# A fifth slot of 1 MB in the experts' weight stream, with the routing tables in the place of the gates

## What is computed

```python
def routed_moe(h, w_router, b_router, w1, w3, w2):
    scores = jax.nn.sigmoid(h @ w_router)
    sel = scores + b_router
    ...
    _, idx = lax.top_k(jnp.where(in_group, sel, -jnp.inf), TOP_K)
    ...
    for e in range(N_EXPERTS):
        y_e = (jax.nn.silu(h @ w1[e]) * (h @ w3[e])) @ w2[e]
        y = y + combine[:, e:e + 1] * y_e
    return y
```

## Time and profile before

| | |
|---|---|
| median of 3 runs | 948.19 us (947.85 to 950.93) |
| the profiled execution | 960.5 us |
| its span, first to last instruction | 958.9 us |
| its mean granted TensorE clock | 0.959 |
| busy PE / PEld / DVE / ACT / POOL | 829.1 / 697.1 / 623.5 / 516.7 / 230.7 us |
| moved by DMA | 209 MB, mean 218 GB/s |

### The profile page before, as it was taken

One profiled execution on the slowest core, in us unless ns is written; L12 is line 12 of the kernel. 1 busy time (PEld: TensorE's weight loads), 2 busy tenths in 40 slices (PEclk: granted clock), 3 DMA queues, 4 the chain that ended last, 5 costly groups with the idle time before them and its releaser, 6 DMA issues. The chain is left out here.

```text
span 958.9 us, 15876 instructions
## 1 busy us (share of the span) xinstructions
PE 829.1 (86%) x6374; PEld 697.1 (73%) x6374; DVE 623.5 (65%) x804; ACT 516.7 (54%) x814; POOL 230.7 (24%) x336
## 2 busy tenths in 40 slices
PE   4998997999889997897879889759999999999980
PEld 2777875898669875697668788648887777777760
DVE  2596764458544676245446465578988888888865
ACT  3475741457323752338343164367777777777751
POOL 3113150124201360013400110007323223223122
PEclk9999999999999999899989999869999999999995
DMA  9977478245943468438694248618999999999964
GB/s 312 268 239 195 123 168 207 62 117 148 211 115 84 137 154 187 117 78 256 184 248 127 67 141 279 242 44 300 340 348 354 360 357 370 372 359 357 339 202 151
DMA packets 220052, 209.00 MB, mean 218 GB/s; under 512 B 51100, under 2 KB 156229, under 8 KB 219337
## 3 DMA queue, kind: packets, MB, share of 16 engines
q1 hardware_dynamic: 217241, 203.80, 68.6%
q0 software_dynamic: 2736, 4.15, 1.3%
HBM read 190.64 MB, written 23.10 MB: 223 GB/s over the span
## 5 line engine op out<-in xcount | busy, mean ns | idle before, releaser
L2038 DVE TENSOR_TENSOR w_lo<-raw,w_hi 128x2048 fp32r<-128x2048 f32 x96 | 232.1, 2428 | 39.4 <-ACT w_hi L1473 39.3
L2259 PE MATMUL bank<-hT,half_hi 128*128 128x256 f32 (+1 forms) x1024 | 228.6, 319 | 10.6 <-DVE half_lo L1593 4.3
L1473 ACT CAST w_hi<-raw 128x2048 fp32r<-128x2048 f32 x96 | 183.3, 1912 | 71.0 <-DMA raw<-in_w_e_dram 65.6
L2259 PEld LDWEIGHTS bank<-hT,half_hi 128*128 128x128 f32 x1024 | 167.2, 192 | 26.9 <-issue 7.8
L2259 PE MATMUL bank<-w_hi,window 128*128 128x512 f32 x480 | 157.7, 399 | 3.0 <-DVE w_lo L2038 3.0
L2259 PE MATMUL bank<-hT,half_lo 128*128 128x256 f32 (+1 forms) x512 | 159.6, 312 | 0.0
L1593 DVE TENSOR_TENSOR half_lo<-half_raw,half_hi 128x1024 fp32r<-128x1024 f32 x88 | 108.6, 1236 | 59.3 <-ACT half_hi L1033 58.8
L2259 PE MATMUL bank<-lane 64*64 64x64 f32 (+2 forms) x2096 | 103.9, 240 | 22.0 <-issue 10.7
L2259 PEld LDWEIGHTS bank<-lane 64*64 64x64 f32 (+2 forms) x2096 | 95.3, 151 | 33.5 <-issue 18.6
L2259 PEld LDWEIGHTS bank<-w_hi,window 128*128 128x128 f32 x480 | 90.2, 188 | 28.0 <-issue 6.6
L1033 ACT CAST half_hi<-half_raw 128x1024 fp32r<-128x1024 f32 x88 | 92.2, 1049 | 26.7 <-DMA half_raw<-in_w_out_dram 8.0
(11 more groups left out here) (321 smaller groups left out, 1285.3 us busy)
## 6 DMA issues: line engine op xcount, KB each, us to landing
raw<-in_w_e_dram SPq DMA_DIRECT2D x96, 1024.0 KB, 7.4
half_raw<-in_w_in_dram SPq DMA_DIRECT2D x64, 512.0 KB, 5.0
half_raw<-in_w_ada_dram SPq DMA_DIRECT2D x32, 512.0 KB, 4.9
raw<-in_w_ada_dram SPq DMA_DIRECT2D x8, 1024.0 KB, 10.7
dense<-staged SPq DMA_DIRECT2D x32, 128.0 KB, 4.4
half_raw<-in_w_proj_a_dram SPq DMA_DIRECT2D x8, 512.0 KB, 5.4
half_raw<-in_w_proj_b_dram SPq DMA_DIRECT2D x8, 512.0 KB, 4.0
half_raw<-in_w_out_dram SPq DMA_DIRECT2D x8, 512.0 KB, 8.7
```

The costliest lines, as they stand in the source:

```text
L1473: act.copy(e_hi[n % WBUF][:, :], raw[n % RING][:, :]).then_inc(s["hi_ready"], 1)
L2038: dve.tensor_tensor(e_lo[n % WBUF][:, :], raw[n % RING][:, :], e_hi[n % WBUF][:, :].bitcast(F32), ALU.subtract)\
L2259: return nc.tensor.matmul(dst, lhsT, rhs, start=start, stop=stop)
```

## The change

The stream gets a fifth slot, `raw4`, of 8 KB on each partition, at the end of the memory. The room for it comes from the routing tables, which now lie over `gates`. In the stream, slot and landing semaphore of unit n are n % 5, SP waits for the split of unit n-5, and the counts of landings follow (`fills_until`). The first ring of eight loads at the kernel's start and the loop for overfull experts still use four slots; the latter's counts are adapted (`turn_fills`).

```diff
--- before.py
+++ after.py
@@ -5,6 +5,7 @@
 
 
 
+import math
 from contextlib import ExitStack
 
 import concourse.bass as bass
@@ -35,6 +36,7 @@
 DE = 512
 N = 512
 RING = 4
+SLOTS_AHEAD = 5
 SLOTS = P
 UNIT = 2048
 HALF = 1024
@@ -120,6 +122,7 @@
         hT_hi, hT_lo = hT[:, 0, :, :], hT[:, 1, :, :]
         ZO_AT = (nc.sbuf_base + 31) // 32 * 32
         zo = sb("zo", [P, 4 * D])
+        GATES_AT = (nc.sbuf_base + 31) // 32 * 32
         gates = sb("gates", [P, 8, TILES, HEADS, DIRS])
         gate_row = sb("gate_row", [P, 2, DIRS, HEADS])
         key_sq = sb("key_sq", [P, 4, TILES])
@@ -175,22 +178,34 @@
         act_hi = sb("act_hi", [P, 4, P], F32R)
         act_lo = sb("act_lo", [P, 4, P], F32R)
         y_out = [sb(f"y_out{g}", [P, D]) for g in range(2)]
-        both = sb("both", [P, 2, EXPERTS], BF16)
...
-        pair_weight = sb("pair_weight", [P, 2, 2])
+        routing_at = GATES_AT
+
+        def sb_routing(name, shape, dt=F32):
+            nonlocal routing_at
+            t = nc.alloc_sbuf_tensor_at(name, shape, dt, offset=routing_at)
+            size = (2 if dt == BF16 else 4) * math.prod(shape[1:])
+            routing_at += (size + 31) // 32 * 32
+            assert routing_at <= GATES_AT + 4 * 8 * TILES * HEADS * DIRS
+            return t
+
+        both = sb_routing("both", [P, 2, EXPERTS], BF16)
...
+        pair_weight = sb_routing("pair_weight", [P, 2, 2])
         y_tok = nc.alloc_sbuf_tensor_at("y_tok", [P, 2, 2, D], F32, offset=LANE_AT)
         window = [nc.alloc_sbuf_tensor_at(f"window{g}", [P, 2, KC, P], F32R, offset=LANE_AT + 8 * D * g) for g in range(2)]
         w_lo4 = nc.alloc_sbuf_tensor_at("w_lo4", [P, UNIT], F32R, offset=VEC_AT + 4 * D)
+        FIFTH_AT = (nc.sbuf_base + 31) // 32 * 32
+        slots = raw + [nc.alloc_sbuf_tensor_at("raw4", [P, UNIT], F32, offset=FIFTH_AT)]
         e_hi = [w_hi3, w_hi[0], w_hi[1], w_hi4]
         e_lo = [w_lo3, w_lo[0], w_lo[1], w_lo4]
 
@@ -319,7 +334,7 @@
             "gathered window_ready rows_placed silu_done act_done act_turned act_rounded act_split "
             "y_copied first_rows x2_ready x2_squared x2_power out_ready"
         ).split()}
-        landed = [sem(f"landed{r}") for r in range(RING)]
+        landed = [sem(f"landed{r}") for r in range(SLOTS_AHEAD)]
         half_landed = [sem(f"half_landed{r}") for r in range(HRING)]
         spilled = [sem(f"spilled{r}") for r in range(STAGES)]
         y_stored = [sem(f"y_stored{g}") for g in range(2)]
@@ -487,6 +502,14 @@
         TURN_AFTER = {3: ("back_copied", 2), 4: ("v_copied", 2), 5: ("k_normed", 3)}
         BACK_AFTER = {0: ("back_copied", 0), 1: ("back_copied", 1), 2: ("k_normed", 4), 3: ("back_copied", 3)}
         SLOT_FILLS = ADA_UNITS // RING
+
+        def fills_until(n):
+            r = n % SLOTS_AHEAD
+            return n // SLOTS_AHEAD + 1 + (SLOT_FILLS if r < RING else 0)
+
+        def turn_fills(k):
+            r = k % RING
+            return SLOT_FILLS + len([n for n in range(ALL_UNITS) if n % SLOTS_AHEAD == r]) + k // RING + 1
         e1_v = w_e1[0].rearrange("e (c p) n -> p (e c) n", p=P)
         e3_v = w_e3[0].rearrange("e (c p) n -> p (e c) n", p=P)
         e2_v = w_e2[0].rearrange("e (c p) n -> p (e c) n", p=P)
@@ -752,7 +775,7 @@
             sp.wait_ge(s["merged_split"], KC)
             def expert_turn(i):
                 for k, (v, q, half) in enumerate(TURN_UNITS):
-                    sp.wait_ge(s["unit_split"], i * PER_TURN + (ALL_UNITS + k - RING + 1))
+                    sp.wait_ge(s["unit_split"], i * PER_TURN + (ALL_UNITS + max(k - RING + 1, 0)))
                     if v is e2_v:
                         src = v[:, bass.ds(i * 8 + q * 4, 4), half * N:half * N + N]
                     else:
@@ -760,13 +783,13 @@
                     load(four(raw[k % RING]), src, landed[k % RING])
 
             for n, (v, q, half_) in enumerate(STREAM):
-                if n >= RING:
-                    sp.wait_ge(s["unit_split"], n - RING + 1)
+                if n >= SLOTS_AHEAD:
+                    sp.wait_ge(s["unit_split"], n - SLOTS_AHEAD + 1)
                 if v is e2_v:
                     src = v[:, 4 * q:4 * q + 4, half_ * N:half_ * N + N]
                 else:
                     src = v[:, 8 * q + 4 * half_:8 * q + 4 * half_ + 4, :]
-                load(four(raw[n % RING]), src, landed[n % RING])
+                load(four(slots[n % SLOTS_AHEAD]), src, landed[n % SLOTS_AHEAD])
             sp.wait_ge(s["h2_ready"], 2)
             load(ada_vec[:, 0, :], final_g.partition_broadcast(P), s["landed_final"])
             last_rows = slice(LISTED, FIRST_TURN)
@@ -1465,12 +1488,12 @@
             x_copy(0, 1)
 
             def expert_high(n):
-                act.wait_ge(landed[n % RING], 16 * (SLOT_FILLS + n // RING + 1))
+                act.wait_ge(landed[n % SLOTS_AHEAD], 16 * fills_until(n))
                 if n < 4:
                     act.wait_ge(s["half_used"], EXPERT_AFTER[n])
                 else:
                     act.wait_ge(s["unit_used"], n - WBUF + 1)
-                act.copy(e_hi[n % WBUF][:, :], raw[n % RING][:, :]).then_inc(s["hi_ready"], 1)
+                act.copy(e_hi[n % WBUF][:, :], slots[n % SLOTS_AHEAD][:, :]).then_inc(s["hi_ready"], 1)
 
             expert_high(0)
             x_squares(1, 0)
@@ -1539,7 +1562,7 @@
             def expert_turn(i):
                 def high(k):
                     act.wait_ge(landed[k % RING], i * (16 * PER_TURN // RING)
-                                + 16 * (SLOT_FILLS + ALL_UNITS // RING + k // RING + 1))
+                                + 16 * turn_fills(k))
                     act.wait_ge(s["unit_used"], i * PER_TURN + (ALL_UNITS + k - WBUF + 1))
                     act.copy(e_hi[k % WBUF][:, :], raw[k % RING][:, :]).then_inc(s["hi_ready"], 1)
 
@@ -2035,7 +2058,7 @@
 
             def expert_low(n):
                 dve.wait_ge(s["hi_ready"], n + 1)
-                dve.tensor_tensor(e_lo[n % WBUF][:, :], raw[n % RING][:, :], e_hi[n % WBUF][:, :].bitcast(F32), ALU.subtract)\
+                dve.tensor_tensor(e_lo[n % WBUF][:, :], slots[n % SLOTS_AHEAD][:, :], e_hi[n % WBUF][:, :].bitcast(F32), ALU.subtract)\
                     .then_inc(s["unit_split"], 1)
 
             def attended(chunk, t):
```

More of the change, by code:

```diff
@@ L177, in block_kernel @@
         y_out = [sb(f"y_out{g}", [P, D]) for g in range(2)]
-        both = sb("both", [P, 2, EXPERTS], BF16)
[L179 to L189, removed]
-        pair_weight = sb("pair_weight", [P, 2, 2])
+        routing_at = GATES_AT
[7 more added lines that the diff above has]
+        both = sb_routing("both", [P, 2, EXPERTS], BF16)
+        pair_at = sb_routing("pair_at", [P, 3, 2])
+        first_of = sb_routing("first_of", [P, 4, EXPERTS])
+        counted = sb_routing("counted", [P, 2, EXPERTS])
+        store_row = sb_routing("store_row", [P, 3, EXPERTS])
+        store_int = sb_routing("store_int", [P, EXPERTS], mybir.dt.int32)
+        first_int = sb_routing("first_int", [P, 2, EXPERTS], mybir.dt.int32)
+        turn_int = sb_routing("turn_int", [P, 2], mybir.dt.int32)
+        second = sb_routing("second", [P, 2, 2, EXPERTS])
+        row_of = sb_routing("row_of", [P, 3, 2, EXPERTS])
+        row_sum = sb_routing("row_sum", [P, 2, 2])
+        row_int = sb_routing("row_int", [P, 2, 4], mybir.dt.int32)
+        pair_weight = sb_routing("pair_weight", [P, 2, 2])
         y_tok = nc.alloc_sbuf_tensor_at("y_tok", [P, 2, 2, D], F32, offset=LANE_AT)
```

## The result

The changed kernel takes 938.99 us in the median of 4 runs (935.7 to 942.4), the kernel before beside it 948.02 us (947.32 to 950.93): 9.0 us less by the medians, whose quotient is 0.990; the ratio worked out from the single runs is 0.988 with a 95% interval of 0.984 to 0.992. In a later comparison, with more runs of both, the medians were 942.43 and 953.62 us, 11.2 us apart, and the ratio was 0.9885 (0.9835 to 0.9935). So the gain is 9 to 11 us, and these runs don't say it closer. The forecast was 939.5 us. Both kernels have a slower state, in which single executions took up to 2076 us; all ratios and intervals here are of fast runs alone.

A forecast was written before the change was run, and what follows sets the result against it. From about 720 us late weight transfers in the experts were taken to set the end. The head start's 2.7 us whole plus 6.0 of the other 9.0 gave 8.7: 948.2 - 8.7 = 939.5 us, range 936.2 to 945.6.

The forecast's parts named there:

- (a): Router's gap: the fifth unit is issued straight behind unit 3, putting the weight stream one unit, 2.7 us, ahead.
- (b): Experts: with five slots the release no longer sets the pace, giving back up to 8.7 us of starved DMA time.
- (c): Experts: no more can be gained than PE's idle 10.9 us plus at most 0.8 us of tail, cap 11.7 us.
- the difference isn't there: Profiled execution, 12.3 us over the median: PE's clock in the experts is 1.00, so the saving carries over to the median.
- (f): Experts: row stores on POOL's queue still slow the stream; DMA's pace 17.6 us per expert against PE's 17.2, some waits remain.
- The round trip: Experts' weight stream: a slot goes round in about 12 us, so four slots give one unit per 3.0 us.
- (d): Routing tables in the place of the gates: only addresses differ, taken as 0, 0.5 us either way at most.
- (e): SP's waits, landing counts and ACT's and DVE's slot index: no added instruction, 0.
- The HBM rival: Experts' weight stream already at HBM's limit, 355 GB/s; only the head start counts, 2.9 us, 945.2 us; chance 0.20.
- The clock rival: Experts: PE without waits is granted a clock of 0.95, 3.5 us longer, 951.7 us; chance 0.06.
- The rival that DVE is the bound: Experts: DVE's splits come as late as before, earlier transfers only lie longer, time stays at 948.2 us; chance 0.06.
- before 720 PE has no such wait: Early experts: until 720 us PE lives on split units in hand, then the weight stream catches it.

The follow-up runs named there:

- experiment 1: Changed kernel, five slots and moved tables kept, but SP waits for the split of unit n-4 (four units ahead): 953.73 us beside 954.91, ratio 1.001.
- experiment 2: Changed kernel with five units ahead only up to unit 11, four from unit 12 on: ratio 0.998 to the kernel before.
- experiment 3: Changed kernel with four units ahead up to unit 11, five from unit 12 on: ratio 0.990 to the kernel before.
- experiment 4: Changed kernel with only three units ahead throughout: 999.35 us, ratio 1.048 to the kernel before.
- experiment 10: Changed kernel with five units ahead up to unit 47, four from unit 48 on: ratio 0.993 to the kernel before.
- experiment 7: Changed kernel (five slots) with the experts' second matmul of three left out, so PE has less work: 932.96 us, ratio 0.978.
- experiment 9: Kernel before with POOL's token-window copies of experts 3 to 15 cut to the first of eight pieces: ratio 0.997.
- experiment 6: Kernel before (four slots) with the experts' second matmul of three left out: ratio 0.997.

## Why the prediction was right, step by step

**The sum** held: 8.7 us forecast, 9.0 measured in the first comparison and 11.2 in the one with more runs. But it was put together wrongly in two of its terms, (a) 2.7 us too high and (b) 3 us or more too low. That these two errors cancelled, wholly by the first comparison and in part by the second, is luck.

**(c), PE's cap**, was right within 0.3 us: PE's need was worked out as 269.0 us and measured as 268.7; an interval as 17.2 and measured as 17.16 to 17.18. The tail went from 2.80 (927.37 to 930.17) to 2.05 us (907.47 to 909.52), 0.75 for the "at most 0.8". In the profiled executions the stage and tail together gave 11.2 + 0.75 = 11.9 us, the whole of the cap of 11.7. Against the first medians' 9.0 that is too much by 3: the profiled execution of before had, with 279.9 us, the longest stage of the depth-four ones (276.9 and 278.2 in experiments 1 and 2, which do the same work), and a longer tail (2.2 and 2.5 us there). So the prediction's "the difference isn't there", said of the 12.3 us by which that execution stood over the median, held for most of them and not for some 3 us, which one trace couldn't show. Against those two executions stage and tail give 8.4 to 10.0, within the 9 to 11 of the medians.

**(a), the head start**, failed: priced at 2.7 us and taken whole, it is worth nothing that was measured by itself (ratio 0.998, 0.995 to 1.001) and 0.3 us within the full change. The step assumed that the stream runs at a fixed rate, so that a unit landed early is a unit ahead to the end. With four slots transfer n is issued when unit n-4 is split, whatever had landed early; and during the first expert those splits are timed by PE (up to 670 us ACT's longer waits name PE and not a landing), so the early unit is in hand for a while and then spent. Within the full change the depth alone already takes the stage to 269.0, and a lead has nothing left to give. The prediction had worked out that a slot's release sets the pace in the paragraph before, and should have applied it here.

**(b), the depth**, failed in size by as much: taken as 6.0 us of a possible 9.0, it gives the whole, 0.990 with no help from the gap (some 9.5 us). The argument for the discount, (f), was that PE wouldn't be quite without waits, since DMA's own pace was put at 17.6 us an expert by scaling busy shares, 1.01 over 1.045. Measured with PE out of the way it is 6 x 2.84 = 17.0 us, under PE's 17.2. The share rose by 3% from before to this run and the rate by 7% (353 to 355, then 379 GB/s), so scaling by the share had the DMA too slow; scaling by the fullest windows, 6 x 2.69 = 16.1 us, would have had it too fast. The stores' bytes, which stood behind (f), cost at most a few tenths of a per cent (0.998).

**The round trip as a cause.** "About 12 us, and four slots then give one unit per 3.0 us" is no second source for ACT's 3.03 us. Each issue follows the release of its slot at once (a split that starts at 661.8 and takes 2.29 us, an issue at 664.1), so the measured round trip over the number of slots is the pace whatever sets it, in the changed kernel too. That the depth was the limit is shown by experiments 1 to 4, which change nothing else.

**(d) and (e)**, nothing for the tables, the semaphores and the waits, were right: 1.001.

**The rivals.** The HBM rival would have left the stream under 360 GB/s; it ran at 375, and at 379 with PE lighter. The Trainium skill, page "DMA: Bandwidth & Descriptors" (Bandwidth), has about 358 GB/s per core as the binding number for transfers from HBM; no run with five slots here is held by it (375 to 379 GB/s), with one core of the chip at work in all of them. The same section of the Trainium skill says that its own single-core measurement is higher (425 GB/s for 16 MB) and that about 358 is what each gets with two cores streaming at once; the rival took the rule without that condition. The clock rival is refuted by a granted clock of 1.00 over the 240 us without a gap. (Its price has a slip: 18.1 against 17.9 us for 15.67 experts is 3.1 us by the figures shown and 3.8 unrounded, not 3.5.) The rival that DVE is the bound is refuted at four slots (ACT waited for landings, and the fifth slot took 11 us off the stage) but isn't far: DVE is busy 96% of the stretch in the light kernel with five.

**The reading "before 720 PE has no such wait"** was right and mattered less than I made of it: it gave experiment 3 its chance to show the full gain without the gap. The expectation of experiment 10 leaned on PE's listed waits for what was lost up to unit 48 and came out too small by half; the transposes' intervals tell it directly.

## What to carry to other kernels

For a ring of buffers, three numbers for one unit are floors of the pace: the consumer's need (here 2.86 us), the transfer with a full queue (between 2.69 us, the fullest windows, and 2.84, experiment 7), and the shortest round trip of a slot, one transfer alone plus all that is done before the slot is free, over the number of slots: (5.0 + 1.9 + 2.3) / 4 = 2.3 us with four, 3.1 with three. The measured paces were 3.03 and 3.55 us, above every floor: transfers that queue behind one another and late releases cost 0.2 us a unit over the highest floor with four slots, and 0.5 with three. So the floors can't clear a ring of being too short, and the round trip read from the trace of the running ring can't either, since over the slots it only restates the pace. What told it was the consumer's chain waiting for landings at a rate (355 GB/s) under that of the fullest windows (389 to 402), and then one run with one slot more or less. A share of 1.01 looked like a full memory and was a ring one slot too short. A head start was worth nothing here, neither where the slots bound nor where PE did; what counts is the depth in the steady state, and it ends at the consumer's need, which a kernel with a third of the consumer's work taken out shows from both sides.

## What the runs showed of the hardware

- A DMA share of 1.01 (a mean over 260 us) still had 6% of rate in it: 355 GB/s with four slots, 375 with five and PE as the bound, 379 with PE lighter. The share is a poor measure of how full the queue is; the time to landing (7.5 against 8.6 us) and the rate told more.
- With nothing to wait for, PE repeats to 0.01 us over 268.68 us in two executions, while three executions with four ahead (before, experiments 1 and 2) scatter by 3 us.
- POOL's copies stretch a split on DVE of 128x2048 from 2.29 to 3.65 us; with copies of an eighth of the size the longest is 2.48 us (experiment 9).
- TensorE's granted clock was lower where PE had gaps: with a third of the experts' matmuls left out and four slots it was 0.93 over 260 us (experiment 6), where it was 1.00 over 260 us of the kernel before; in experiment 7, with shorter gaps, it was 0.99.
- With three, four and five slots a transfer of 1 MB landed in 6.0, 7.5 and 8.6 us in the median, at 303, 355 and 375 GB/s.
